# All prompt tiles' residual rows read ahead of the experts' rows, the sample by quarters on GpSimd's queue, the first and last tile summed in PSUM

## The reference

```python
x = x + mix @ p['w_out']                  # the residual rows, x2 in the kernel
x = x + _moe(_rmsnorm(x, p['norm2_g']), p)   # + cw[0] * expert A's row + cw[1] * expert B's row
y = x * rsqrt(mean(x * x) + EPS) * final_norm_g
```

## Time and profile before

| what | value |
|---|---|
| time, median of 3 runs | 737.05 us |
| lowest and highest | 735.68 and 737.68 us |
| the profiled execution, its time | 734.72 us |
| the profiled execution, its span | 733.0 us |
| busy PE, DVE, ACT, POOL | 89%, 34%, 22%, 13% |
| HBM read, written | 235.65 MB, 19.20 MB |
| DMA queue q1 (SP), share of 16 engines | 77.1% |

### The profile page before, as it was taken

How to read it: one execution, slowest core, us unless ns; L and a number is a source line. 1 busy time by engine, 2 the same in 40 slices (tenths; PEclk the granted TensorE clock), 3 DMA queues, 4 the chain that set the end, 5 groups by cost and what they waited for, 6 DMA issues and landing times.

```text
span 733.0 us, 9145 instructions
## 1 busy us (share of the span) xinstructions
PE 652.5 (89%) x3164; PEld 314.2 (43%) x3164; DVE 251.0 (34%) x516; ACT 161.5 (22%) x317; POOL 95.4 (13%) x161
## 2 busy tenths in 40 slices
PE   8999999999998899996899999877878776778995
PEld 4478888874455533332233333322222222223331
DVE  7798997187266520101010111100000100001057
ACT  3677511232432111110011111101000101001033
POOL 5100000000000212122012122211211112111000
PEclk9999999999999899997899999999999999999998
DMA  9533005469736899999999999999999999999983
GB/s 326 218 115 114 3 1 203 170 256 430 284 118 258 323 412 425 426 421 421 429 426 424 425 425 421 424 423 427 424 424 426 427 424 425 427 424 423 417 344 121
DMA packets 30004, 246.52 MB, mean 336 GB/s; under 512 B 6064, under 2 KB 6576, under 8 KB 16896
## 3 DMA queue, kind: packets, MB, share of 16 engines
q1 hardware_dynamic: 23216, 233.95, 77.1%
q0 software_dynamic: 5280, 8.21, 3.1%
q10 hardware_dynamic: 1456, 3.62, 1.3%
HBM read 235.65 MB, written 19.20 MB: 348 GB/s over the span
## 4 chain that ended last, share of the span: by engine, by line
PE 48%; DMA 36%; DVE 10%; ACT 3%; issue 2%; SPq 0%; POOLq 0%; POOL 0%; DVEq 0%
PE psA L1407 25%; DMA mem<-in_w_gu 25%; PE psB L1407 21%; DMA mem<-in_w_down 7%; DVE mem L731 4%; DMA mem<-hn_d,mem 2%; DVE mem L955 1%; DMA mem<-in_w_vb 1%; ACT front_c L665 1%; DMA hn_d<-front_c 1%; DVE mem L870 1%; ACT mem L673 1%; DVE mem L882 1%; PE psA L1412 1%; DVE mem L912 1%
## 5 line engine op out<-in xcount | busy, mean ns | idle before, releaser
L1407 PE MATMUL psA<-mem 128*64 128x512 f32 (+8 forms) x1368 | 309.0, 515 | 26.5 <-DMA mem<-in_w_gu 16.4
L1407 PE MATMUL psB<-mem 128*64 128x512 f32 (+7 forms) x1210 | 267.1, 540 | 31.6 <-DMA mem<-in_w_gu 20.3
L1407 PEld LDWEIGHTS psA<-mem 128*64 128x64 f32 (+4 forms) x1368 | 142.3, 151 | 174.4 <-issue 126.3
L1407 PEld LDWEIGHTS psB<-mem 128*64 128x64 f32 (+3 forms) x1210 | 109.0, 152 | 172.5 <-issue 123.0
L731 DVE TENSOR_TENSOR mem<-mem 128x512 f32<-128x512 f32 (+17 forms) x116 | 67.6, 597 | 23.7 <-ACT mem L565 19.6
L1163 DVE TENSOR_TENSOR front_c<-front_c,psA 64x512 f32<-64x512 f32 x15 | 10.3, 690 | 175.8 <-ACT front_c L665 175.8
L1163 DVE TENSOR_TENSOR front_c<-front_c,psB 64x512 f32<-64x512 f32 x15 | 10.3, 690 | 171.3 <-ACT front_c L665 171.3
L1325 POOL DMA_INDIRECT y_d<-front_c,mem x30 | 30.8, 1028 | 268.3 <-ACT front_c L676 268.3
L1320 POOL DMA_INDIRECT mem<-hn_d,mem x34 | 36.0, 1058 | 94.6 <-DMA hn_d<-front_c 65.4
L665 ACT ACTIVATE front_c<-psA 64x512 f32<-64x512 f32 x15 | 8.8, 589 | 121.6 <-PE psA L1407 121.6
L665 ACT ACTIVATE front_c<-psB 64x512 f32<-64x512 f32 x15 | 8.8, 589 | 115.3 <-PE psB L1407 115.3
(11 more groups left out here) (246 smaller groups left out, 365.3 us busy)
## 6 DMA issues: line engine op xcount, KB each, us to landing
mem<-in_w_gu SPq DMA_DIRECT2D x63, 2048.0 KB, 33.4
mem<-in_w_down SPq DMA_DIRECT2D x31, 2048.0 KB, 37.6
mem<-in_w_out SPq DMA_DIRECT2D x2, 2048.0 KB, 8.4
y_d<-mem SPq DMA_DIRECT2D x1, 4096.0 KB, 11.8
mem<-y_d SPq DMA_DIRECT2D x8, 512.0 KB, 8.4
mem<-in_x_T SPq DMA_DIRECT2D x8, 260.0 KB, 8.8
mem<-in_w_vb SPq DMA_DIRECT2D x8, 256.0 KB, 8.9
mem<-in_x_prompt SPq DMA_DIRECT2D x4, 512.0 KB, 11.2
```

The source lines that it names most:

```text
L1407: return nc.tensor.matmul(out, lhsT, rhs, start=start, stop=stop, skip_group_check=True)
```

## The change

- SP issues the residual rows of all four prompt tiles before it waits for `rest_out`, and after it the experts' rows of tiles 0 to 3.
- The sample's 8 rows are laid out as 32 quarter rows: quarter q of row i on partition 32q + i, 256 columns. Its residual rows and the gain are loaded early, by eight small DMAs behind `load(20)`; its experts' rows come by two gathers of GpSimd, and its result leaves by a scatter of GpSimd. The sum of squares of the four quarters is added across partitions by four small matmuls (`same_row`). GpSimd clears the places and VectorE builds `same_row` and the weights `cwq` between experts' tiles early on.
- Order in the tail: additions of tiles 0, 1, 2, 3, sample; tiles 0 and 3 are summed in PSUM instead of 0 and 1, and tile 3's product and norm come last.

The core of the diff:

```diff
@@ -211,11 +211,16 @@
...
-        picks = view(20480, NTOK)
+        picks = view(20480, NP_ + 32)
...
+        WQ = D // 4
+        xq, yq0, yq1, gfq = (view(16384 + WQ * k, WQ) for k in range(4))
+        cwq, sumq, rootq, scaleq = tiny[:, 20:22], tiny[:, 22:23], tiny[:, 23:24], tiny[:, 24:25]
+        same_row = st[:, 0:32]
+        quarter_rows = sb("quarter_rows", [128, 3], i32)
...
@@ -269,9 +274,9 @@
...
-        LAST_ORDER = (0, 1, 4, 2, 3)
-        LAST_PS = [psA[:, 0:2, :], psA[:, 2:4, :], psB[:, 0:2, :], psA[:, 0:2, :], psB[0:NS, 2:4, :]]
-        IN_PSUM = (0, 1)
+        LAST_PS = [psA[:, 0:2, :], psA[:, 2:4, :], psB[:, 0:2, :], psA[:, 0:2, :], psB[:, 2, 0:D // 4]]
+        ROW_SUMS = psB[:, 3, 0:1]
+        IN_PSUM = (0, 3)
...
@@ -419,6 +428,12 @@
...
+                if q == 2 * NSLOT:
+                    sp.wait_ge(tokens_rdy, 2)
+                    for k in range(4):
+                        at = slice(32 * k, 32 * k + NS)
+                        sp.dma_start(gfq[at], a["final_norm_g"][WQ * k:WQ * k + WQ].unsqueeze(0).to_broadcast([NS, WQ])).then_inc(rest_in, 16)
+                        sp.dma_start(xq[at], x2_d[NP_:NTOK, WQ * k:WQ * k + WQ]).then_inc(y_in[4], 16)
...
@@ -426,22 +441,20 @@
...
-            for t in LAST_ORDER[0:3]:
+            for t in range(4):
                 residual(t)
             sp.wait_ge(rest_out, 1)
             for u in range(2):
                 sp.wait_ge(y_out[u], 16 * (NE // 2 - 1))
-            for n, t in enumerate(LAST_ORDER):
-                if n >= 3:
-                    residual(t)
+            for t in range(4):
                 for c in range(2):
                     r0 = c * NTOK + t * 128
                     sp.dma_start(yin[0:ROWS[t], 2 * t + c, :], y2_d[r0:r0 + ROWS[t], :]).then_inc(y_in[t], 16)
-            for n, t in enumerate(LAST_ORDER):
-                sp.wait_ge(f_done, n + 1)
-                dst = o[0][0, t * 128:(t + 1) * 128, :] if t < 4 else o[1].rearrange("b l d -> (b l) d")
-                sp.dma_start(dst, x2[0:ROWS[t], t, :]).then_inc(f_out, 16)
-            sp.wait_ge(f_out, 16 * NT)
+            for t in range(4):
+                sp.wait_ge(f_done, t + 1 if t < 3 else NT)
+                sp.dma_start(o[0][0, t * 128:(t + 1) * 128, :], x2[:, t, :]).then_inc(f_out, 16)
+            sp.wait_ge(f_out, 16 * 4)
+            sp.wait_ge(y_out[0], 16 * (NE // 2))
...
@@ -703,17 +716,23 @@
...
+            def root_of_sum(t, total):
+
+                A(halves(yin[:, 2 * t, :]), total, ACT.Square, accum_out=fx[:, t:t + 1]).then_inc(f_sq, 1)
+                act.wait_ge(f_sq, t + 1 if t == 0 else t + 2)
+                A(ss[:, 2, t:t + 1], fx[:, t:t + 1], ACT.Sqrt, scale=1.0 / D, bias=epsc[:, :]).then_inc(f_rt, 1)
+
+            act.wait_ge(f_ps, 1)
+            root_of_sum(0, LAST_PS[0])
+            act.wait_ge(f_sum, 1)
+            A(yq0, xq, ACT.Square, accum_out=sumq).then_inc(f_sq, 1)
+            for t in (1, 2):
+                act.wait_ge(f_sum, t + 1)
+                root_of_sum(t, halves(x2[:, t, :]))
+            act.wait_ge(f_ps, 5)
+            A(rootq, ROW_SUMS, ACT.Sqrt, scale=1.0 / D, bias=epsc[:, :]).then_inc(f_rt, 1)
+            act.wait_ge(f_ps, 6)
+            root_of_sum(3, LAST_PS[3])
...
@@ -1194,10 +1213,15 @@
...
+            dve.wait_ge(tokens_rdy, 2)
+            V.tensor_reduce(same_row, ident[:, :].rearrange("p (q r) -> p r q", q=4), AX.X, ALU.add)
+            for q in range(4):
+                ins = V.tensor_copy(cwq[32 * q:32 * q + NS], cw[0:NS, :, 4])
+            ins.then_inc(picks_rdy, 1)
...
@@ -1214,44 +1238,50 @@
...
             def add_rows(t):
-                r = ROWS[t]
-                dve.wait_ge(y_in[t], 48)
+
+                dve.wait_ge(y_in[t], 48 if t < 4 else 64)
+                if t == 4:
+                    dve.wait_ge(xg_in[0], 16 * (NE // 2 + 1))
+                    dve.wait_ge(xg_in[1], 16 * (NE // 2 + 1))
+                acc, rows, by = ((x2[:, t, :], yin[:, 2 * t:2 * t + 2, :], cw[:, :, t]) if t < 4
+                                 else (xq, view(16384 + WQ, 2, WQ), cwq))
                 for j in range(2):
-                    ins = V.scalar_tensor_tensor(x2[0:r, t, :], yin[0:r, 2 * t + j, :], cw[0:r, j, t:t + 1], x2[0:r, t, :],
-                                                 ALU.mult, ALU.add)
+                    ins = V.scalar_tensor_tensor(acc, rows[:, j], by[:, j:j + 1], acc, ALU.mult, ALU.add)
                     if j == 0:
                         link(ins)
                 ins.then_inc(f_acc, 1)
...
-            for t in LAST_ORDER:
+            for t in range(4):
                 add_rows(t)
...
+            dve.wait_ge(picks_rdy, 2)
+            add_rows(4)
+
+            def add_kept(t, count):
+
+                dve.wait_ge(f_ps, count)
+                dve.wait_ge(f_acc, t + 1)
+                total = halves(x2[:, t, :]) if t < 4 else xq
+                tt(total, total, LAST_PS[t], ALU.add).then_inc(f_sum, 1)
+
+            def scaled(t, count):
+
+                dve.wait_ge(f_rt, count)
+                link(V.reciprocal(ss[:, 3, t:t + 1], ss[:, 2, t:t + 1]))
+                V.scalar_tensor_tensor(halves(x2[:, t, :]), LAST_PS[t] if t in IN_PSUM else halves(x2[:, t, :]), ss[:, 3, t:t + 1],
+                                       halves(gfb), ALU.mult, ALU.mult).then_inc(f_done, 1)
+
+            add_kept(4, 2)
+            dve.wait_ge(rest_in, 16 * 9)
+            scaled(0, 1)
+            add_kept(1, 3)
+            add_kept(2, 4)
+            scaled(1, 2)
+            scaled(2, 3)
+            dve.wait_ge(f_rt, 4)
+            link(V.reciprocal(scaleq, rootq))
+            V.scalar_tensor_tensor(xq, xq, scaleq, gfq, ALU.mult, ALU.mult).then_inc(f_done, 1)
+            scaled(3, 5)
...
@@ -1301,6 +1331,10 @@
...
+            pool.wait_ge(consts, 5)
+            for c in range(3):
+                for q in range(4):
+                    link(G.iota(quarter_rows[32 * q:32 * q + 32, c:c + 1], [[0, 1]], base=4 * (c * NTOK + NP_ if c < 2 else 0) + q, channel_multiplier=4))
...
@@ -1384,6 +1418,10 @@
...
+            pool.wait_ge(x2_out, 16 * NT)
+            G.memset(view(16384, 4 * WQ), 0.0)
+            G.memset(picks[:, NTOK:NP_ + 32], 0.0)
+            G.memset(cwq, 0.0).then_inc(tokens_rdy, 1)
...
@@ -1399,6 +1437,16 @@
...
+            for u in range(2):
+                pool.wait_ge(y_out[u], 16 * (NE // 2 - 1))
+            for c in range(2):
+                G.indirect_dma_start(out=(yq0, yq1)[c], out_offset=None, in_=y2_d.rearrange("t (q n) -> (t q) n", q=4),
+                                     in_offset=bass.IndirectOffsetOnAxis(ap=quarter_rows[:, c:c + 1], axis=0),
+                                     bounds_check=8 * NTOK - 1, oob_is_err=False).then_inc(xg_in[c], 16)
+            pool.wait_ge(f_done, 4)
+            G.indirect_dma_start(out=o[1].rearrange("b l (q n) -> (b l q) n", q=4),
+                                 out_offset=bass.IndirectOffsetOnAxis(ap=quarter_rows[:, 2:3], axis=0),
+                                 in_=xq, in_offset=None, bounds_check=4 * NS - 1, oob_is_err=False).then_inc(y_out[0], 16)
...
@@ -1818,29 +1866,38 @@
...
+            def kept(t, halves=(0, 1)):
+
+                for h in halves:
+                    if t == 0:
+                        pe.wait_ge(y_last, 3 + h)
+                    ins = mm(LAST_PS[t][:, h, :], picks[:, 128 * t:128 * t + 128], y_kept[:, 512 * h:512 * h + 512], t not in IN_PSUM, True)
+                ins.then_inc(f_ps, 1)
+
+            pe.wait_ge(tokens_rdy, 2)
+            pe.wait_ge(picks_rdy, 2)
...
             rest(0)
             pe.wait_ge(y_last, 2)
-            kept(0, 0)
-            rest(1)
-            kept(1, 1)
-            kept(2, LAST_ORDER[2])
-            kept(3, LAST_ORDER[3])
+            kept(0)
+            for q in range(4):
+                ins = mm(LAST_PS[4][32 * q:32 * q + 32], picks[:, NP_:NP_ + 32], y_kept[:, WQ * q:WQ * q + WQ], True, True)
+            ins.then_inc(f_ps, 1)
+            kept(1)
+            kept(2)
             pe.wait_ge(f_done, 1)
-            kept(4, LAST_ORDER[4])
+            rest(3)
+            pe.wait_ge(f_sq, 2)
+            for q in range(4):
+                ins = mm(ROW_SUMS[32 * q:32 * q + 32], same_row, sumq, True, True)
+            ins.then_inc(f_ps, 1)
+            kept(3)
...
```

More of the change, by code:

```diff
@@ L322, in build, with halves @@
         own = {0: psA[:, 2:4, :], 1: psB[:, 0:2, :], 2: psB[:, 2:4, :], 3: psA[:, 2:4, :], 4: psA[:, 0:2, :]}
+        def halves(v):
+            return v.rearrange("p (a n) -> p a n", a=2)
         def stored(eng, n, u):
@@ L1226, in add_rows @@
                 ins.then_inc(f_acc, 1)
-            for t in LAST_ORDER:
+            for t in range(4):
                 add_rows(t)
-            def add_kept(n, t):
-                dve.wait_ge(f_ps, n + 1)
-                dve.wait_ge(f_acc, n + 1)
-                x2t = x2[0:ROWS[t], t, :].rearrange("p (a n) -> p a n", a=2)
```

(36 more changed lines are left out.)

3 lines of the change are left out of this document (1 added, 2 removed).

## The result

The changed kernel takes 738.86 us (median of 20 runs, 737.58 to 741.20) where the kernel before took 736.61 in the same session (20 runs, 734.49 to 739.05). The ratio is 1.0027, 95% interval 1.0017 to 1.0038: slower, by 2.2 us. The forecast was 736.7, no change. The profiled execution of after was timed at 738.16 us and spans 736.4, against 734.72 and 733.0 of before.

A forecast was written before the change was run, and what follows sets the result against it. Weights were taken to bound the middle, and landings then VectorE the tail. Terms of -0.4 behind 718.8, 0 before and -0.3 to +1.1 for packets gave 736.7 us against the median; range 733.8 to 739.3.

The forecast's parts named there:

- POOL's part: GpSimd in the tail: gathers land by 709; final scatter issued at 728.1 lands at 731.2, 1.0 ahead: free.
- rival (c): Kernel's end: the final scatter, landing 5 to 7.7 us after the sample's scaling, ends it; say 738.5; chance 0.12.
- (d): Small packets or a stall at tile 1 cost 1 to 3 us: 738 to 740; chance 0.08.
- The residual rows first: Tail transfers: first addition at 708.1 instead of 705.6, last landing still 716.2, additions end at 718.8 as today.
- Rival (b): Tail transfers: filling the trough brings the last landing 2.5 us earlier, to 713.7; 734.1 us; chance 0.18.
- What bounds the tail of the kernel before: Tail: bound by VectorE from 708.63 on, and by landings just before.
- The sample by quarters: VectorE's sample work in the tail falls from 5.2 to 2.1 us, saving 3.1, partly in the stretch waiting for landings.
- VectorE behind the additions: Tail behind 718.8: 10.76 us instead of 11.17, including 0.40 idle; VectorE ends 0.4 earlier, at about 729.6.
- TensorE: Tail: quarter products 0.43 to 1.72 us, small sums 0.3; tile 3 in PSUM ready in time, with thin covers.
- The early part: Early setup on POOL and VectorE is free, hidden in idle time or waits; small DMAs add 0.15 to 0.5 us.

The follow-up runs named there:

- b1: Kernel before plus a one-column memset on GpSimd at the very end, released by the last scaling: 738.88 us, ratio 1.0029.
- b4: Kernel before plus a one-column memset on GpSimd, released by the third scaling: 736.70 us, ratio 0.9991.
- b5: Kernel before plus a one-column memset on GpSimd, released by the fourth scaling: 737.39 us, ratio 1.0009.
- a1: Changed kernel with the sample's result stored by four small SP DMAs instead of GpSimd's scatter: 736.39 us, ratio 0.9998 to the kernel before.
- b2: Kernel before with only SP's transfer order changed, all residual rows ahead of the experts' rows: 738.80 us, ratio 1.0020.
- b3: Kernel before with only the final norm's gain read early, right behind load(7): 736.50 us, ratio 1.0000.
- c2: Changed kernel with the sample stored by SP and scaled before tile 1: 735.88 us, ratio 0.9995 to the kernel before.
- c3: Changed kernel, sample stored by SP and scaled before tile 1, final gain read early, residuals 2 and 3 late: 736.96 us, ratio 0.9997 to before.
- a2: Changed kernel, GpSimd's scatter kept, with the sample scaled before tile 1: 737.01 us, ratio 1.0000 to the kernel before.
- c1_again: Repeat of the best version: changed kernel, sample stored by SP and scaled before tile 1, final gain read early: 734.34 us, ratio 0.9965 to before.
- c3_again: Repeat of c3 on the same chip as c1_again: 737.00 us, ratio 0.9997 to the kernel before.

## Why the prediction was wrong

**The step that failed is POOL's part.** It weighed the final scatter by its landing alone (728.1 + 3.1 = 731.2, "1.0 ahead: free"). Two things were off. The smaller: from VectorE's release at 728.65 to the scatter's start at 729.48 lie 0.83 us in GpSimd's sequencer, and with the landing of 3.5 its data came at 732.9, not 731.2. That is 4.3 behind the scaling, just past the 4.1 from which rival (c) decides, and is worth 0.2 to 0.3: SP waits 2.6 us at its end for the scatter, where it waits 2.3 for its own last store in before. The larger: behind its last instruction GpSimd has a DRAIN of 5.6 to 5.7 us, which the sum doesn't hold. It was in the trace of before, 5.6 us long at 698.9; I had read GpSimd's timeline, which leaves out the sequencer's own instructions, and not the listing of L45. The right bound was: GpSimd's last instruction end + 5.7 against SP's last landing, so in after anything of it that ends later than 733.2 - 5.7 = 727.5 costs. b1, b4 and b5 show this, and a1 that nothing else made the kernel slower. Rival (c), a landing 5 to 7.7 us behind the sample's scaling, did not happen (4.3); its sign, the scatter as the last landing, did show by the 0.2 to 0.3. Its size, 738.5, is near the measured 738.86 by luck, and so is that the measured time lies within 733.8 to 739.3: the upper part of that range was meant for (c) and (d).

**The residual rows first: right.** Expected: first addition at 708.1, then the pace of the landings, the last at 716.2, end at 718.8. Measured: first at 709.45 (708.9 with W moved back by 0.5), then eight in one run to 719.64 (719.1). The first is 0.8 later than expected, by as much as the scatter took longer to land (8.5 against 7.7). Behind it VectorE has no idle time, but no slack either. In a1, which has the same order of transfers, this is the last transfer of experts' rows:

```profile
L452 SPq DMA_DIRECT2D mem<-y_d x1: 489/489/489, 703.7 to 703.7; - x1
...
DMA to landing us min/median/max: 13.2/13.2/13.2
```

It lands at 716.9, or 715.9 with a1's W moved back to that of before, and VectorE, from 709.43 at 2.54 a tile, wants it at 717.05. In after itself the last packets move past 716:

```profile
716.00:717.00 1.00, 1.00 (x10) 0.39 (x3) 1.00 (x1) 1.00 (x2) 0.00 (x0) 1.00 0.04 16
```

So the landings set the pace as forecast, and the additions end 39.9 behind W against 39.6 before. The price of the order, 2.6 for tile 0's additions pushed behind the others, and the gain of 2.6 for the sample's full-sized additions cancel; b2 shows the first by itself. Rival (b), with the last landing at 713.7 and 2.5 us gained, fell.

**What bounds the tail of the kernel before: incomplete.** The prediction put it down to VectorE and the landings alone. TensorE's sum of tile 1 comes in level with them, as b3 showed. It did not touch the forecast, since the change takes tile 1 out of PSUM.

**The sample by quarters: right.** Two additions 1.00, kept rows 0.42, scaling 0.48 and 0.15; expected 1.0, 0.43, 0.48 and 0.16. **VectorE behind the additions: right.** From 719.55 to 730.01 it is 10.46, expected 10.76; the idle time before the scaling of tile 1 was 0.42, expected 0.40. **TensorE: right.** Its timeline in after:

```profile
715.80 0.64 PE L1455 MATMUL psB<-front_c,mem 128*32 128x256 f32 x8
...
722.53 1.98 PE L1455 MATMUL psA<-mem,ident 128*128 128x512 f32 x4 [2.45 <-DVE mem L1271]
724.44 0.24 PE L1455 MATMUL psB<-tiny,st 128*32 128x1 f32 x8
```

The products took 0.64 (bounds 0.43 and 1.72), the sums 0.24 (taken at 0.3), and the last scaling waited for none of them.

**The early part: right.** VectorE's new sum and copies (0.38 and 0.67 at 259 us) left 1.64 of the wait of the earlier trace rows standing. **Small packets (d):** not the cause of the loss, since W is within what it is elsewhere and a1, with as many small transfers, is not slower than before; whether they cost a few tenths is not told by these runs.

## What to carry to other kernels

Before an instruction is put at the end of an engine that was idle there, list what that engine does behind its last instruction until the final barrier: on GpSimd it is 5.6 us, so by these runs its last work must end at least that long before the last store lands. Two edits of one change can each be worth nothing or less and pay together, since one takes away what hides the other: here the residual rows first and the gain read early made 0.3% together, and neither of them anything that the runs can tell without the other (c2, c3). Where an edit that should pay gives nothing, look for a second holder that comes in level with the first (b3). Compare tails from a fixed event of the same trace, here the end of the weight stream, since its place varies more from run to run than the effect measured.

## What the runs showed of the hardware that I had not expected

- GpSimd's DRAIN at the end of the program lasts 5.59 to 5.61 us behind a memset (before, b1, b4, b5) and ends 5.7 us behind the end of a scatter on its engine (after, a2). Where its last instructions were gathers whose data landed late, it ended 2.8 us behind the last landing: in c1_again the landing was at 711.0 and the DRAIN, begun at 704.0, ended at 713.8; in a1 712.1 behind 709.2.
- TensorE's granted clock fell to 0.50 in the tail for some 3.5 us (c3_again, c2) after it had been idle 1.1 to 1.25 us, had done eight matmuls of one column and had been idle 0.61 more. In a2 it had been idle 1.40 and 0.61 us around the same eight, and in after 2.45 us at once, and the clock stayed at 1.00 in both. What decides is open.
- The last scatter of the experts' rows lands 7.3 to 8.5 us after issue, behind the stream, with either order of the residual rows. While the experts' rows wait for it, the DMA engines move 74 (c3_again) to 254 GB/s (b2) in the emptiest microsecond of each version. No run tried to shorten it.
